# Expert groups of 112 places in place of 128, without the unused last gather, in a two-layer encoder trunk

## The reference, cut to what matters

```python
D_MODEL, N_EXPERTS, N_GROUPS, EXPERTS_PER_GROUP, TOP_K, D_EXPERT = 1024, 16, 4, 4, 2, 256
...
def _swiglu(x, wg, wu, wd):
    return (jax.nn.silu(x @ wg) * (x @ wu)) @ wd

def _moe(x, router_w, router_b, wg, wu, wd, sg, su, sd):
    ...
    s = jax.nn.sigmoid((xf @ router_w).astype(jnp.float32))
    sb = s + router_b.astype(jnp.float32)
    gscore = jnp.sum(lax.top_k(sb.reshape(-1, N_GROUPS, EXPERTS_PER_GROUP), TOP_K)[0], axis=-1)
    gsel = jnp.argmax(gscore, axis=-1)
    emask = (jnp.arange(N_EXPERTS) // EXPERTS_PER_GROUP)[None, :] == gsel[:, None]
    _, idx = lax.top_k(jnp.where(emask, sb, -jnp.inf), TOP_K)
    wsel = jnp.take_along_axis(s, idx, axis=-1)
    wsel = wsel / jnp.sum(wsel, axis=-1, keepdims=True)
    gate = jnp.sum(jax.nn.one_hot(idx, N_EXPERTS, dtype=jnp.float32) * wsel[..., None], axis=1)
    out = _swiglu(xf, sg, su, sd).astype(jnp.float32)
    for e in range(N_EXPERTS):
        out = out + gate[:, e:e + 1] * _swiglu(xf, wg[e], wu[e], wd[e]).astype(jnp.float32)
```

## Time and profile before

| | us |
|---|---|
| median of 3 runs (1057.86 to 1059.55) | 1059.23 |
| the profiled execution, whole | 1059.46 |
| its span | 1057.7 |
| PE busy | 1011.2 |
| DVE busy | 827.4 |
| ACT busy | 661.5 |

### The profile page before, as it was taken

How to read it: one execution, slowest core, us unless ns; L and a number is a source line. 1 busy time by engine, 2 the same in 40 slices (tenths; PEclk the granted TensorE clock), 3 DMA queues, 4 the chain that set the end, 5 groups by cost and what they waited for, 6 DMA issues and landing times. The chain is left out here.

```text
span 1057.7 us, 24596 instructions
## 1 busy us (share of the span) xinstructions
PE 1011.2 (96%) x10118; PEld 777.8 (74%) x10118; DVE 827.4 (78%) x1488; ACT 661.5 (63%) x1059; POOL 0.7 (0%) x10
## 2 busy tenths in 40 slices
PE   6999999999999999999999999999999989999995
PEld 4777777777776799975467777777777768999552
DVE  4786677654799899999887776676548989999986
ACT  5565454854355788786767445457543668887864
POOL 0000000000000000000000000000000000000000
PEclk9999999999999999999999999999999999999998
DMA  9754443423464399998735534443234426999971
GB/s 349 276 181 131 155 130 125 135 84 111 149 221 141 102 321 330 323 328 318 275 121 193 154 121 147 144 126 116 91 126 152 155 80 205 324 329 330 349 257 52
DMA packets 59653, 205.06 MB, mean 194 GB/s; under 512 B 7088, under 2 KB 10348, under 8 KB 59020
## 3 DMA queue, kind: packets, MB, share of 16 engines
q1 hardware_dynamic: 55980, 195.96, 53.7%
q10 hardware_dynamic: 3552, 7.42, 2.0%
HBM read 198.77 MB, written 3.40 MB: 191 GB/s over the span
## 5 line engine op out<-in xcount | busy, mean ns | idle before, releaser
L1049 DVE SCALAR_TENSOR_TENSOR wlo<-w,whi 128x1024 f16<-128x1024 f32 x358 | 429.3, 1220 | 60.7 <-ACT whi L549 58.7
L549 ACT ACTIVATE whi<-w 128x1024 f16<-128x1024 f32 x358 | 370.4, 1049 | 81.3 <-PE bank L1755 48.1
L1755 PE MATMUL bank<-xhi,whi 128*128 128x320 f16 x688 | 206.6, 300 | 0.0
L1755 PE MATMUL bank<-xlo,whi 128*128 128x320 f16 x688 | 206.0, 299 | 0.0
L1755 PE MATMUL bank<-xhi,wlo 128*128 128x320 f16 x688 | 205.9, 299 | 0.0
L1755 PE MATMUL bank<-arena_b,whi 128*128 128x128 f16 x2048 | 179.5, 219 | 0.0
L1755 PE MATMUL bank<-arena_b,wlo 128*128 128x128 f16 x1024 | 175.3, 219 | 0.0
L1755 PEld LDWEIGHTS bank<-arena_b,whi 128*128 128x128 f16 x2048 | 157.1, 98 | 0.9 <-issue 0.9
L1755 PEld LDWEIGHTS bank<-arena_b,wlo 128*128 128x128 f16 x1024 | 100.2, 98 | 0.0
L1755 PEld LDWEIGHTS bank<-xhi,whi 128*128 128x128 f16 x688 | 67.3, 98 | 29.9 <-issue 2.5
L1755 PEld LDWEIGHTS bank<-xhi,wlo 128*128 128x128 f16 x688 | 67.4, 98 | 26.3
(11 more groups left out here) (369 smaller groups left out, 1763.1 us busy)
## 6 DMA issues: line engine op xcount, KB each, us to landing
w<-in_w SPq DMA_DIRECT2D x358, 512.0 KB, 4.7
arena_b<-head_rows ACTq DMA_DIRECT2D x2, 1920.0 KB, 6.9
xT<-in_x SPq DMA_DIRECT2D x2, 640.0 KB, 4.6
out_y<-xT SPq DMA_DIRECT2D x4, 320.0 KB
rows<-in_rows ACTq DMA_DIRECT2D x1, 1024.0 KB, 11.2
rows<-in_rows SPq DMA_DIRECT2D x1, 1024.0 KB, 5.7
out_ckv<-arena_a SPq DMA_DIRECT2D x2, 320.0 KB
acc<-kr SPq DMA_DIRECT2D x2, 288.0 KB
```

The lines of the kernel that those rows point to most:

```text
L549: A(whi[:, n % SLOTS, :], w32[:, n % RAW, :], ACT.Copy, scale=WS).then_inc(hi_done.sem, 1)
L1049: V.scalar_tensor_tensor(wlo[:, n % SLOTS, :], w32[:, n % RAW, :], WS, whi[:, n % SLOTS, :], ALU.mult, ALU.subtract).then_inc(lo_done.sem, 1)
L1755: ins = M(out, w[:, s, sub * P:(sub + 1) * P], rhs(part, k), start=(n == 0), stop=(n == 3 * len(subs) - 1))
```

## The change

`CAP` becomes 112. With it shrink the zeros and ones, the gathered tokens, the gate rows, the matmuls of the expert blocks and the steps of DVE and ACT on the hidden values (224 columns in place of 256), and the memory laid out for them. In the down projection the standing operand has 112 columns; the results of a group have 112 partitions. A layer in which a group has over 112 tokens takes the general way. The fifth group of zeros, its memset, its gathers in group 3 and their copies go. The core of the diff:

```diff
@@ -70,7 +70,7 @@
-CAP = P
+CAP = 112
...
-        one_hot = f16_a[:, ONE0:ONE0 + (GROUPS + 1) * 3 * CAP]
-        OT0 = ONE0 + (GROUPS + 1) * 3 * CAP
+        one_hot = f16_a[:, ONE0:ONE0 + GROUPS * 3 * CAP]
+        OT0 = ONE0 + GROUPS * 3 * CAP
...
-        x_grp = f16_b[:, HEND:HEND + 2 * 4 * 512].rearrange(
+        x_grp = f16_b[:, HEND:HEND + 2 * 2 * KD * CAP].rearrange(
...
-                    A(gate_hi[0:EXPERTS, :], bank[4][0:EXPERTS, :], ACT.Copy).then_inc(g_hi.sem, 1)
+                    A(gate_hi[0:EXPERTS, :], bank[4][0:EXPERTS, 0:GROUPS * CAP], ACT.Copy).then_inc(g_hi.sem, 1)
+                    def next_rows(e, b, a, e2):
+
+                        act.wait_ge(xg_ps.sem, xg_ps.value(l, e + 5))
+                        A(x_grp[:, b, a, 4 * e2:4 * e2 + 4, :], bank[5][:, 0:4 * CAP]
+                          .rearrange("p (k n) -> p k n", k=4), ACT.Copy).then_inc(xg_ev.sem, 1)
+
...
-                            A(slot_tok[:, bass.ds((gg * 2 + g2) * T, T)], bank[7][:, 0:T], ACT.Copy,
+                            A(slot_tok[0:CAP, bass.ds((gg * 2 + g2) * T, T)], bank[7][0:CAP, 0:T], ACT.Copy,
...
-                                    act.wait_ge(xg_ps.sem, xg_ps.value(l, e + 5))
-                                    A(f16_b[:, bass.ds(qq * 1024 + (e2 * 512 + HEND + (1 - g2) * 2048),
-                                                       512)], bank[5][:, :], ACT.Copy
-                                      ).then_inc(xg_ev.sem, 1)
+                                    if e < EXPERTS - PER_GROUP:
+                                        next_rows(e, 1 - g2, qq, e2)
...
-                V.memset(one_hot[:, GROUPS * 3 * CAP:], 0.0)
...
                     for c in range(4):
                         for i in range(3):
-                            a = M(bank[b][:, c * P:(c + 1) * P],
+                            a = M(bank[b][:, c * CAP:(c + 1) * CAP],
...
-                                        if j == 1:
+                                        if j == 1 and g < GROUPS - 1:
...
-                        pe.wait_ge(xg_ev.sem, xg_ev.value(l, 20))
+                        pe.wait_ge(xg_ev.sem, xg_ev.value(l, 4 * GROUPS))
...
-                                    a = M(b[:, :], h_[:, bass.ds(g * (8 * CAP) + ((2 * q + kt) * CAP + H0),
+                                    a = M(b[0:CAP, :], h_[:, bass.ds(g * (8 * CAP) + ((2 * q + kt) * CAP + H0),
...
-                                      slot_tok[:, g * T:(g + 1) * T], start=False,
+                                      slot_tok[0:CAP, g * T:(g + 1) * T], start=False,
```

More of the change, by code:

```diff
@@ L360, in build_trunk @@
         gt_l = sig("gt_l", 1)
-        xg_ps = sig("xg_ps", 20)
-        xg_ev = sig("xg_ev", 20)
+        xg_ps = sig("xg_ps", 4 * GROUPS)
+        xg_ev = sig("xg_ev", 4 * GROUPS)
         ot_ps = sig("ot_ps", GROUPS)
@@ L930, in _ @@
                         act.wait_ge(xg_ps.sem, xg_ps.value(l, q + 1))
-                        A(x_grp[:, 0, q // 2, 4 * (q % 2):4 * (q % 2) + 4, :], bank[5 + q % 2][:, :]
+                        A(x_grp[:, 0, q // 2, 4 * (q % 2):4 * (q % 2) + 4, :], bank[5 + q % 2][:, 0:4 * CAP]
                           .rearrange("p (k n) -> p k n", k=4), ACT.Copy).then_inc(xg_ev.sem, 1)
@@ L976, in group_out @@
                         act.wait_ge(blk_done.sem, blk_done.value(l, g * 4 + ((D0, D1)[hf] + 5)))
-                        A(y_hi[:, bass.ds(g * 512, 512)], bank[(4, 2)[hf] + g2][:, :], ACT.Copy,
+                        A(y_hi[0:CAP, bass.ds(g * 512, 512)], bank[(4, 2)[hf] + g2][0:CAP, :], ACT.Copy,
                           scale=UN * XS).then_inc(yg_hi.sem, 1)
@@ L1000, in _ @@
                 with act.Else():
-                    for s_, n in ((xg_ev, 20), (ot_ev, GROUPS), (yg_hi, 2 * GROUPS), (e_tanh, EXPERTS),
+                    for s_, n in ((xg_ev, 4 * GROUPS), (ot_ev, GROUPS), (yg_hi, 2 * GROUPS), (e_tanh, EXPERTS),
                                   (e_hi, EXPERTS)):
@@ L1648, in _ @@
                     dve.wait_ge(g_hi.sem, g_hi.value(l, 1))
-                    V.tensor_tensor(gate_lo[0:EXPERTS, :], bank[4][0:EXPERTS, :], gate_hi[0:EXPERTS, :],
+                    V.tensor_tensor(gate_lo[0:EXPERTS, :], bank[4][0:EXPERTS, 0:GROUPS * CAP], gate_hi[0:EXPERTS, :],
                                     ALU.subtract).then_inc(g_lo.sem, 1)
@@ L1694, in group_out @@
                         dve.wait_ge(yg_hi.sem, yg_hi.value(l, g + (4 * hf + 1)))
-                        V.scalar_tensor_tensor(y_lo[:, bass.ds(g * 512, 512)],
-                                               bank[(4, 2)[hf] + g2][:, :], UN * XS,
-                                               y_hi[:, bass.ds(g * 512, 512)], ALU.mult, ALU.subtract
+                        V.scalar_tensor_tensor(y_lo[0:CAP, bass.ds(g * 512, 512)],
+                                               bank[(4, 2)[hf] + g2][0:CAP, :], UN * XS,
+                                               y_hi[0:CAP, bass.ds(g * 512, 512)], ALU.mult, ALU.subtract
                                                ).then_inc(yg_lo.sem, 1)
@@ L2217, in gate_slots @@
                         for part in (gt_hi, gt_lo):
-                            a = M(bank[4][0:EXPERTS, :], part[:, i, :], slots[:, :, i, :],
+                            a = M(bank[4][0:EXPERTS, 0:GROUPS * CAP], part[:, i, :], slots[:, :, i, :],
                                   start=(i == 0 and part is gt_hi), stop=(i == 2 and part is gt_lo))
@@ L2240, in _ @@
                                 t0, n = TILES[i]
-                                a = M(bank[7][:, t0:t0 + n],
+                                a = M(bank[7][0:CAP, t0:t0 + n],
                                       one_hot[:, bass.ds(g * (3 * CAP) + i * CAP, CAP)],
@@ L2301, in scatter @@
                             for y in (y_hi, y_lo):
-                                a = M(bank[banks[i]][:, 0:T], y[:, g * 512 + i * P:g * 512 + (i + 1) * P],
-                                      slot_tok[:, g * T:(g + 1) * T], start=False,
+                                a = M(bank[banks[i]][:, 0:T], y[0:CAP, g * 512 + i * P:g * 512 + (i + 1) * P],
+                                      slot_tok[0:CAP, g * T:(g + 1) * T], start=False,
                                       stop=(g == last and y is y_lo))
@@ L2331, in _ @@
                 with pe.Else():
-                    pe.sem_inc(xg_ps.sem, 20)
+                    pe.sem_inc(xg_ps.sem, 4 * GROUPS)
                     pe.sem_inc(ot_ps.sem, GROUPS)
```

## The result

The kernel with groups of 112 places takes **1052.29 us** (median of 4 runs, 1051.31 to 1053.35), the kernel before 1059.39 in the same series (4 runs, 1057.86 to 1059.82). The ratio is 0.9936, with a 95% interval of 0.9919 to 0.9953: faster by 0.64%, about 7 us, where 6.9 were forecast (1052.4). The profiled execution took 1053.35 us with a span of 1051.6; before it was 1059.46 and 1057.7. Lines 1672, 1676, 1680 and 1687 of before are 1675, 1679, 1683 and 1690 now; L1755 is L1758, L2286 is L2289, L2316 is L2319, L1695 is L1698, L1049 is L1053, and ACT's L971 and L943 are L975 and L949. One execution of the kernel after, in the series of e0_again, took 1071.71 us at a mean clock of 0.944 and is left out of the ratios.

A forecast was written before the change was run, and what follows sets the result against it. The prediction took a 6.27 us loop per expert through DVE and ACT as the bound, with PE just behind. Terms of 4.0, 2.0, 0.4 and 0.5 us sum to 6.9, giving 1052.4 us, range 1050.3 to 1056.5.

The forecast's parts named there:

- The loop: Expert stage: narrower DVE steps and ACT copy save 0.125 us an expert, 4.0 us in all.
- The boundaries: Group boundaries: narrower matmuls let PE arrive in time, removing one DVE wait; 0.40 us at five boundaries, 2.0 us.
- The first down block: Start of the down stage: without the last gather PE arrives sooner; some 0.2 us a layer, 0.4 us in all.
- Routing: Ahead of the experts: comparisons and L1649 on DVE lose columns, 0.5 us together.
- The down stage: Down projection: PE sets the pace at 512 columns a matmul, narrower weight load covered; gain set at nothing.
- The rival with that load as its mechanism: Down stage, 384 matmuls: the 112-wide weight load shows; at 18 ns each the gain is spent, slower from 24; 5%.
- PE as the wall: Expert stage: matmuls of 112 columns repeat like those of 128; 1.6 us a layer gained, 1056.1 us; 11%.
- The general way: A group holds over 112 tokens, so one layer takes the slower general path: 1221 us; 3%.
- The clock: Last group: PE stands a fifth of the time; 10 us at half speed lose 5 us, 1057.4 us; 6%.

The follow-up runs named there:

- e0_again: The changed kernel with no edit, timed again beside the kernel before: 1051.76 us without the execution of 1071.71, ratio 0.9936.
- e4_pe_wide: Changed kernel, but the 96 matmuls of an expert's blocks stream 128 columns and gathers are copied at 512; DVE's steps keep 224: 1053.69 us, ratio 0.9950.
- e3_dve_wide: Changed kernel, but DVE's first two steps of each expert and ACT's tanh work on 256 columns in place of 224: 1055.17 us, ratio 0.9961.
- e9_hi_early: Changed kernel with slot_tok copied late, and ACT making the next expert's first weight block before copying the product's high half: 1049.86 us, ratio 0.9911.
- e8_copy_late: Changed kernel, but ACT copies slot_tok late in the group's first expert, not at the start of a group: 1050.35 us, ratio 0.9917.
- e1_drop_only: Changed kernel with groups of 128 places again, so only the fifth gather, its copies and its memset are dropped: 1058.43 us, ratio 0.9996.
- e5_still_128: Changed kernel, but the down stage loads 128 stationary columns again, the 16 further ones unused: 1052.28 us, ratio 0.9935.
- e2_narrow_only: Changed kernel with 112 places, but the fifth gather of zeros and its copies kept: 1052.89 us, ratio 0.9940.
- e7_cap104: Changed kernel with groups of 104 places, so layer 1 takes the general way and layer 2 stays compact; one run: 1238.07 us.
- e6_cap120: Changed kernel with groups of 120 places in place of 112: 1055.75 us (median of 9), ratio 0.9972.

## Why the prediction was right

**The bound.** The loop through DVE and ACT was read from the order of their instructions, not from the page, where PE is ahead. e4_pe_wide and e3_dve_wide bear it out: wide columns in PE's blocks cost 1.2 us in the stages, on two DVE steps and the tanh 2.2. e9_hi_early shows directly that the loop closes over ACT's high half: nothing is computed less there, only ACT's order is changed, and each expert is 0.06 us shorter. That also says how little ACT's part holds up: DVE's own work is 6.08 of the 6.14 us. That the medians differ by 7.1 us where 6.9 were forecast is partly luck: the stages give 6.45, with one term of 0.4 nearly empty and a loss of 0.28 not foreseen.

**The loop, 0.125 us an expert (4.0 us).** 6.27 became 6.14. By pieces, the three steps gave 0.03, 0.04 and 0.02, and ACT's way from L975 to its next block 0.04 (0.33 to 0.29), where I had 0.105 for the steps and 0.02 for ACT. The sum was right, the shares a little off. ACT's price was read from unlike instructions: L943 is a copy of 320 columns, L959 a tanh of 256, while the copy of 256 (L971) lasts 0.42 us like that of 320.

**The boundaries, 0.40 us at five (2.0 us).** 0.72 became 6.47 - 6.14 = 0.33, with the one wait left that was named. The size holds, and so does the exception: at layer 2's first boundary, behind DVE's pause, 0.37 us became 0.33. The reason given, narrower matmuls, holds at two of layer 1's three boundaries, with less to spare than forecast: 0.56 us saved against ACT's 0.40 should have left 0.16, and the tanh starts 0.05 us behind PE's third block (e8_copy_late shows PE late again as soon as ACT is earlier); at the third the dropped gather does it as well (e1_drop_only). The prediction looked for the gather's worth only behind the last expert, in the wrong place, and the overlap with the narrow matmuls hid that.

**The first down block, 0.4 us: this step failed.** It gave 0.04. PE's timeline of the kernel before where the third bank's matmuls begin, chain of waits of the kernel after, and DVE's timeline over the same piece:

```profile
985.30 0.30 PE L2316 MATMUL bank<-arena_a,wlo 128*128 128x320 f16 x1
985.43 0.30 PE L2316 MATMUL bank<-arena_a,whi 128*128 128x320 f16 x1
985.57 0.30 PE L2316 MATMUL bank<-arena_b,whi 128*128 128x320 f16 x1
```

```profile
979.18 1.80 PE bank L2319 x12
980.99 12.96 PE bank L2289 x60
```

```profile
978.74 0.39 DVE L1679 TENSOR_TENSOR mk<-mk,bank 128x224 f32<-128x224 f32 x1
...
981.79 0.38 DVE L1690 SCALAR_TENSOR_TENSOR arena_b<-mo,arena_a 128x224 f16<-128x224 f32 x1
982.17 5.11 DVE L1053 SCALAR_TENSOR_TENSOR wlo<-w,whi 128x1024 f16<-128x1024 f32 x4
987.20 0.68 DVE L1698 SCALAR_TENSOR_TENSOR arena_b<-bank,arena_b 112x512 f16<-112x512 f32 x1
```

The bank is free at 978.74 + 0.39 = 979.13, and PE's second half starts at 979.18. That much was seen. But its records end 1.86 us behind the release, not 1.63; before it was 987.23 - 985.31 = 1.92. PE was already held close to that release: before, the thirteenth matmul started at 985.43, 0.12 behind it and in step with the others, and after, 0.05 behind it. So only 0.07 us were there to gain. My 0.29 came from setting 987.23, the end of the last record, against twelve matmuls at their distance (12 x 0.136 = 1.63), which leaves out that the last record lasts 0.30 us. And it wouldn't have helped: from the last L1690 on DVE works without a pause through four weight blocks up to the first L1698 (0.38 + 5.03 = 5.41 us), and those are the same in both kernels.

**Routing, 0.5 us.** 0.33 and 0.26 up to L1675 of the first expert, 0.6 in all.

**The down stage, 0 us.** It lost 0.28 us in the two layers. 0.2 of it is the longer weight load behind a stop of PE, which e5_still_128 takes away. The rest, 0.08 in the first half of layer 2, goes with the dropped gather and not with the narrow load: from the first to the fourth L1698 of layer 2 the kernel before and e2_narrow_only, which keep the gather, need 15.54 us, while e1_drop_only (128 columns), e5_still_128 and the kernel after need 15.62. By which wait is not shown. The rival with that load as its mechanism had the mechanism in part right and the size wrong by far: the record of the load is longer by 32 ns, not by 5, yet the matmuls of 512 columns cover it everywhere but at their restart. The Trainium skill, page "TensorE: Matmul & The Clock Gate", section "Weight-path perf modes", gives the fast weight load to loads of 128 columns alone; 130 against 98 ns agrees in direction, and 130 ns are over before 512 columns have streamed (216 ns).

**The rivals.** PE as the wall falls: 0.049 us a matmul at 112 columns. The same page's section "Back-to-back issue gap" has about 81 ns at 128 columns in a stream that reloads its weights; no run here came near it. The general way did not happen, and e7_cap104 shows where it would have: 1238 and not 1221. The clock kept 1.00 in the last group.

**Left open.** In layer 2 DVE stands some 0.45 us before a step of the last expert ahead of the first boundary, in the kernel before as in the kernel after, where it stands before L1683, without a cause that the trace shows. It adds 0.37 us to that expert. The trace of e5_still_128 lacks it.

## What to carry to other kernels

Where three resources are busy over 90% of a stage, write down the loop that closes on itself, start by start, across the engines; its length against each engine's own work tells what a cut is worth on each. Work taken from the engine just behind the loop is worth only the waits it causes where it is late, at group boundaries here, and two edits that take away the same wait must not both be credited. Before counting an earlier finish, look whether the consumer has work of its own up to the moment it reads.

## What the runs showed of the hardware

The record of a float16 weight load of 128 stationary columns lasts 98 ns. Narrower ones go up by about 0.42 ns a column and pass it: 16 columns 90 ns (before), 64 columns 110, 104 columns 127 (e7_cap104), 112 columns 130 (after), 120 columns 133 (e6_cap120). So 128 stationary columns load faster than 112. Hidden behind 512 streamed columns the 112-wide load cost 0.04 us at each restart of PE.

Matmuls with a load for each start 0.049 us apart at 112 streamed columns, 0.0558 at 128, 0.136 at 320 and 0.216 at 512.

The granted clock falls to 0.50 for about 3.4 us at one or two places in most of the profiled executions (577 and 854 us in that of the kernel after, 577 alone in e0_again, 338 alone in e3_dve_wide) and nowhere from 14 to 1044 us in that of e6_cap120; one such place was there in one execution and not in another of the same kernel. The kernel before took 1057.6 to 1058.8 us at a mean clock of 0.995 or 0.996, 1058.9 to 1059.9 at 0.994 and 1060.9 to 1061.4 at 0.992 (39 runs); the kernel with 120 places ran from 1053.96 to 1058.39 at 0.997 to 0.991. Effects below 1 us can't be told from that by a total, but they can by the distance of two instructions within the trace. The stages repeated to 0.03 us, but for the pause of DVE in layer 2, which is worth 0.4 us and is missing in one trace.
